# Down stage of the feed-forward parts: a block of the product in seven products in place of eight

## The reference, cut to what matters

```python
D_MODEL, SEQ, DEPTH, D_FF = 1024, 512, 2, 2816

def swiglu(x, w_gu, w_down):
    g, u = jnp.split(x @ w_gu, 2, axis=-1)
    return (jax.nn.silu(g) * u) @ w_down

for layer in range(DEPTH):
    f = swiglu(rmsnorm(h, g[N_FFN1_PRE]), ffn_w_gu[layer, 0], ffn_w_down[layer, 0])
    h = h + 0.5 * rmsnorm(f, g[N_FFN1_POST])
    # ... even layer: sparse attention and RG-LRU; odd layer: gated linear attention
    # ... cross-attention to 256 memory tokens
    f = swiglu(rmsnorm(h, g[N_FFN2_PRE]), ffn_w_gu[layer, 1], ffn_w_down[layer, 1])
    h = h + 0.5 * rmsnorm(f, g[N_FFN2_POST])
```

## Time and profile before

| | us |
|---|---|
| median of 3 runs | 2181.17 (2180.8 to 2181.19) |
| the profiled execution, its own time | 2181.75 |
| its span | 2180.0 |
| TensorE busy (PE) | 2163.3 |
| VectorE busy (DVE) | 1453.7 |
| ScalarE busy (ACT) | 1130.1 |
| GpSimd busy (POOL) | 110.4 |
| mean granted TensorE clock | 0.999 |

### The profile page before, as it was taken

The page is one execution under the profiler, slowest core; times in us unless marked ns, Lnnn a source line. Parts: engine busy times, 40 slices in busy tenths (PEclk is TensorE's granted clock), DMA queues, the critical chain, the costliest instruction groups (busy, mean ns, idle before and its releaser), DMA issues.

```text
span 2180.0 us, 36486 instructions
## 1 busy us (share of the span) xinstructions
PE 2163.3 (99%) x13768; PEld 1944.7 (89%) x13768; DVE 1453.7 (67%) x2179; ACT 1130.1 (52%) x1887; POOL 110.4 (5%) x104
## 2 busy tenths in 40 slices
PE   9999999999999999999999999999999999999998
PEld 8999888775888899998899998898889889999987
DVE  8888635798565688874388886354356567888732
ACT  6555534476554555554365555245445546555531
POOL 0000000576000000000000000000000000000000
PEclk9999999999999999999999999999999999999999
DMA  4332332221452233323323333323323422333332
GB/s 165 106 106 96 116 99 71 78 72 55 135 165 78 78 115 98 105 95 118 126 70 104 106 106 106 106 75 104 103 77 120 155 82 74 102 103 103 115 97 78
DMA packets 62017, 221.51 MB, mean 102 GB/s; under 512 B 7985, under 2 KB 8113, under 8 KB 61922
## 3 DMA queue, kind: packets, MB, share of 16 engines
q1 hardware_dynamic: 57456, 208.69, 29.4%
q10 hardware_dynamic: 4466, 11.53, 1.5%
HBM read 218.09 MB, written 2.10 MB: 101 GB/s over the span
## 4 chain that ended last, share of the span: by engine, by line
PE 91%; DVE 5%; ACT 2%; DMA 1%; POOL 1%; issue 1%; DVEq 0%; POOLq 0%; ACTq 0%
PE ps L2116 12%; PE ps L2118 12%; PE ps L2117 12%; PE ps L2212 11%; PE ps L2214 11%; PE ps L2213 11%; PE ps L481 6%; PE ps L482 5%; PE ps L483 5%; PE ps L2052 1%; DMA w_raw<-in_wstream 1%; DVE w_lo L419 1%; DVE e_sc L1776 1%; DVE e_max L1775 1%; DVE e_sc L1791 1%
## 5 line engine op out<-in xcount | busy, mean ns | idle before, releaser
L419 DVE TENSOR_TENSOR w_lo<-w_raw,w_hi 128x1024 fp32r<-128x1024 f32 x204 | 252.2, 1240 | 350.9 <-ACT w_hi L414 349.9
L414 ACT ACTIVATE w_hi<-w_raw 128x1024 fp32r<-128x1024 f32 x210 | 221.7, 1057 | 322.3 <-PE ps L2214 216.9
L2116 PE MATMUL ps<-t_hi,w_hi 128*128 128x256 f32 x1280 | 362.3, 283 | 0.0
L2118 PE MATMUL ps<-t_hi,w_lo 128*128 128x256 f32 x1280 | 362.3, 283 | 0.0
L2117 PE MATMUL ps<-t_lo,w_hi 128*128 128x256 f32 x1280 | 362.3, 283 | 0.0
L2118 PE MATMUL ps<-x_hi,w_lo 128*128 128x256 f32 x960 | 271.7, 283 | 0.0
L2117 PE MATMUL ps<-x_lo,w_hi 128*128 128x256 f32 x960 | 271.7, 283 | 0.0
L2116 PE MATMUL ps<-x_hi,w_hi 128*128 128x256 f32 x960 | 271.7, 283 | 0.0
L1498 DVE TENSOR_TENSOR w_lo<-f,w_hi 128x1024 fp32r<-128x1024 f32 x152 | 186.1, 1224 | 124.2 <-ACT w_hi L841 124.2
L481 PE MATMUL ps<-x_hi,w_hi 128*128 128x256 f32 (+1 forms) x736 | 250.7, 341 | 2.0 <-DVE x_lo L1375 1.0
L482 PE MATMUL ps<-x_lo,w_hi 128*128 128x256 f32 (+1 forms) x736 | 246.0, 334 | 0.0
(11 more groups left out here) (358 smaller groups left out, 4308.1 us busy)
## 6 DMA issues: line engine op xcount, KB each, us to landing
w_raw<-in_wstream SPq DMA_DIRECT2D x310, 512.0 KB, 3.7
w_raw_odd<-in_wstream SPq DMA_DIRECT2D x80, 512.0 KB, 3.6
tmp<-in_post_gains ACTq DMA_DIRECT2D x8, 512.0 KB, 4.5
gain_bc<-in_gains ACTq DMA_DIRECT2D x7, 512.0 KB, 3.8
h<-in_x SPq DMA_DIRECT2D x4, 512.0 KB, 6.2
c_mem<-in_mem ACTq DMA_DIRECT2D x2, 1024.0 KB, 5.5
out_dram<-h SPq DMA_DIRECT2D x3, 512.0 KB, 2.7
c_gain<-in_mem_gains ACTq DMA_DIRECT2D x2, 512.0 KB, 7.6
```

The lines of the kernel that those rows point to most:

```text
L414: nc.scalar.activation(weights(v)[0], raw(v), ACT.Copy).then_inc(w_hi_ready, 1)
L419: nc.vector.tensor_tensor(wl, raw(v), wh.bitcast(f32), ALU.subtract).then_inc(w_ready, 1)
L2116: nc.tensor.matmul(dst, wh[:, at], xh[:, b, :], start=first, stop=False, skip_group_check=True)
L2118: last = nc.tensor.matmul(dst, wl[:, at], xh[:, b, :], start=False, stop=final, skip_group_check=True)
```

## The change

In the Down stage, the first eight of the 22 inner tiles, with all 512 tokens and all 1024 columns, are seen as a product of 2x2 blocks: 256 tokens by four inner tiles, times four inner tiles by 512 columns. The four blocks of the result come from seven block products (Strassen's scheme in Winograd's form) in place of eight. Each block product has two units of 12 products. The other 14 inner tiles stay as before, as row units. `DOWN` is the order of the 28 units; 14 of them are loaded as before and split, four (of products 1 and 2) too, and the ten of products 3 to 7 are made from blocks that lie in the space of `x_hi` and `x_lo`, which the gate/up stage no longer needs.

VectorE makes the sums of weights (`first_t`, `t_second`, `t_third`, `t_fourth`), the sums of activations (`a_raw`) and the lower parts of both. Products 1, 5, 6 and 7 are copied by ScalarE out of PSUM into `f` (`down_kept`), since they go into two results; VectorE adds them to other banks (`put`). SP loads six block units, two of them ahead of unit 0. `output` is no longer used for the Down stage; each engine has a `down` of its own. Half 0 now ends ahead of the three late units of half 1.

```diff
+BLOCKS = {1: (0, 0), 2: (0, 1), 3: (1, 1)}
+DOWN = [("block", n, k) for n in (1, 2, 5) for k in range(2)] + [("row", 1, 4)]
+DOWN += [("block", 6, 0), ("block", 6, 1), ("row", 1, 5), ("block", 7, 0), ("block", 7, 1), ("row", 1, 6)]
+DOWN += [("block", 3, 0), ("block", 3, 1), ("row", 1, 7), ("block", 4, 0), ("block", 4, 1)]
+DOWN += [("row", 0, q) for q in range(4, FT // 2)] + [("row", 1, q) for q in range(8, FT // 2)]
+DOWN_FIRST = DOWN.index(("row", 0, FT // 2 - 1)) + 1
...
-    "ffn": [("gate_up", 2 * FT), ("down", FT)],
+    "ffn": [("gate_up", 2 * FT), ("down", len(DOWN))],
...
+                        places = (DOWN.index(("block", 4, 1)), DOWN.index(("block", 3, 1)), DOWN.index(("row", 0, 5)))
+                        LAST_USE.append(U[i, seg] + places[late] if kind == "ffn" else U[i, "v"] + KT - 1)
...
         def _(sp):
...
+                            if at == ("block", 1, 0):
+                                sp.wait_ge(w_free, U[i, "gate_up"] + 2 * PLAIN + 2)
+                                for k in range(2):
+                                    sp.dma_start(x_quarter(*AT12, k), block_rows(i, FT // 2 + k)).then_inc(block_in[0], 16)
+                            elif at == ("block", 5, 0):
+                                sp.wait_ge(w_free, U[i, seg] - 2 + 3)
+                                for k in range(2):
+                                    sp.dma_start(x_quarter(*AT22, k), block_rows(i, FT // 2 + 2 + k)).then_inc(block_in[1], 16)
+                            elif at == ("row", 1, 5):
+                                sp.wait_ge(prod, 5 * (SEVENS[i] + FT))
+                                for k in range(2):
+                                    sp.dma_start(x_quarter(*AT21, k), block_rows(i, 2 + k)).then_inc(block_in[2], 16)
...
         def _(act):
...
-                act_upper(i, 0)
+                form_upper(i, 1)
                 keep(it, par, K1, 0, 0)
...
+                form_upper(i, 2)
                 split_hi(act, d0 + 2)
                 pair_silu(it, par)
                 act.wait_ge(w_free, d0 + 2)
-                act_upper(i, 1)
                 split_hi(act, d0 + 3)
-                output(i, "down", FT // 2)
+                down(i)
...
+            def down_kept(i, n):
+
+                act.wait_ge(w_free, U[i, "down"] + DOWN.index(("block", (1, 5, 6, 7)[n], 1)) + 3)
+                b = 0 if n == 1 else 6
+                nc.scalar.activation(kept_place(n), ps[:, b:b + 2, :], ACT.Copy).then_inc(d_kept, 1)
+
+            def down_upper(i, p):
+
+                v = U[i, "down"] + p
+                what, n, k = DOWN[p]
+                if what == "row" or n < 3:
+                    split_hi(act, v)
+                    return
+                if n == 3:
+                    act.wait_ge(block_in[1], 32 * (nffn[i] + 1))
+                else:
+                    act.wait_ge(w_sum, 8 * nffn[i] + W_SUMS[n] + k + 1)
+                act.wait_ge(w_free, LAST_USE[v] + 3)
+                nc.scalar.activation(weights(v)[0].rearrange("p (a b) -> p a b", b=HB), x_quarter(*T_PLACE[n], k),
+                                     ACT.Copy).then_inc(w_hi_ready, 1)
+
+            def down(i):
+                act.preload_act_table(ACT.Sqrt)
+                act.wait_ge(w_free, d0 + 2)
+                act.wait_ge(a_sum, 4 * nffn[i] + A_SUMS[5])
+                form_upper(i, 5)
...
+                for p in range(len(DOWN)):
+                    if p == 1:
+                        down_kept(i, 0)
+                        act_upper(i, 4)
+                    elif p == 3:
+                        act.wait_ge(a_sum, 4 * nffn[i] + A_SUMS[6])
+                        form_upper(i, 6)
+                    elif p == 5:
+                        down_kept(i, 1)
+                        act_upper(i, 5)
+                        act.wait_ge(a_sum, 4 * nffn[i] + A_SUMS[7])
+                        form_upper(i, 7)
...
+                    if p == DOWN_FIRST - 1:
+                        for t in range(TT):
+                            post_square(i, 0, t)
+                    if p + AHEAD < len(DOWN):
+                        down_upper(i, p + AHEAD)
+                    elif d0 + p + AHEAD < NU:
+                        split_hi(act, d0 + p + AHEAD)
...
         def _(dve):
...
-                act_lower(i, 0)
+                form_lower(i, 1)
+                dve.wait_ge(prod, 5 * (s0 + FT) - 4)
+                dve.wait_ge(block_in[0], 32 * (nffn[i] + 1))
+                first_t(i, 0)
                 split_lo(dve, d0)
                 dve.wait_ge(gu_free, n0 + FT + 1)
                 gate_first(it, 1)
+                first_t(i, 1)
                 split_lo(dve, d0 + 1)
                 up_second(it, 1)
                 gate_second(it, 1)
+                form_lower(i, 2)
                 split_lo(dve, d0 + 2)
                 pair_mul(it, 1)
-                act_lower(i, 1)
+                dve.wait_ge(gu_free, n0 + FT + 2)
+                nc.vector.tensor_tensor(a_raw(5), a_block(1, 0), a_block(1, 1), ALU.add).then_inc(a_sum, 1)
                 split_lo(dve, d0 + 3)
-                output(i, "down", FT // 2)
+                down(i)
...
+            def down(i):
...
+                def t_second():
+                    dve.wait_ge(block_in[1], 32 * (nffn[i] + 1))
+                    dve.wait_ge(w_ready, d0 + DOWN.index(("block", 5, 1)) + 1)
+                    for k in range(2):
+                        t = x_quarter(*T_PLACE[6], k)
+                        nc.vector.tensor_tensor(t, x_quarter(*AT22, k), t, ALU.subtract).then_inc(w_sum, 1)
...
+                def put(b, n):
+                    part = ps[:, b:b + 2, :]
+                    nc.vector.tensor_tensor(part, part, kept_place(n), ALU.add).then_inc(d_sum, 1)
+
+                for p in range(len(DOWN)):
+                    if p == 0:
+                        form_lower(i, 5)
+                    elif p == 2:
+                        dve.wait_ge(a_sum, 4 * nffn[i] + 1)
+                        nc.vector.tensor_tensor(a_raw(7), a_block(0, 0), a_block(1, 0), ALU.subtract).then_inc(a_sum, 1)
+                        dve.wait_ge(a_sum, 4 * nffn[i] + 2)
+                        nc.vector.tensor_tensor(a_raw(6), a_raw(5), a_block(0, 0), ALU.subtract).then_inc(a_sum, 1)
+                        act_lower(i, 4)
+                    elif p == 3:
+                        t_second()
+                        form_lower(i, 6)
+                    elif p == 4:
+                        t_third()
+                    elif p == 5:
+                        act_lower(i, 5)
...
+                    if p == DOWN_FIRST - 1:
+                        half_sums(i)
+                        for t in range(TT):
+                            store_half(i, 0, t)
+                    if p + AHEAD < len(DOWN):
+                        down_lower(i, p + AHEAD)
+                    elif d0 + p + AHEAD < NU:
+                        split_lo(dve, d0 + p + AHEAD)
...
         def _(pe):
...
+                def block_part(n, k, start):
+                    v = d0 + DOWN.index(("block", n, k))
+                    pe.wait_ge(w_ready, v + 1)
+                    wh, wl = weights(v)
+                    hi, lo = a_form(n)
+                    for t in range(2):
+                        for j in range(2):
+                            at = slice(j * SEQ, (j + 1) * SEQ)
+                            ah, al = (a[:, 2 * k + j, t * P:(t + 1) * P] for a in (hi, lo))
+                            last = added(bank(banks[n] + t), ah, al, wh[:, at], wl[:, at], start and k == j == 0)
+                    last.then_inc(w_free, 1)
...
+                block_product(1, True)
+                block_product(2, True)
+                pe.wait_ge(gu_free, n0 + FT + 2)
+                block_product(5, True)
+                pe.wait_ge(d_kept, 4 * nffn[i] + 2)
+                row(1, 4, (2, 3, 0, 1), (2, 3))
+                block_product(6)
+                row(1, 5, range(TT))
+                pe.wait_ge(d_kept, 4 * nffn[i] + 3)
+                block_product(7)
+                row(1, 6, range(TT))
+                block_product(3)
+                row(1, 7, range(TT))
+                pe.wait_ge(d_kept, 4 * nffn[i] + 4)
+                block_product(4)
+                pe.wait_ge(d_sum, 4 * nffn[i] + 1)
+                for q in range(4, FT // 2):
+                    row(0, q, range(TT))
+                pe.wait_ge(d_sum, 4 * nffn[i] + 4)
+                pe.wait_ge(w_ready, d0 + len(DOWN))
+                for t in range(TT):
+                    for q in range(8, FT // 2):
+                        last = row_tile(1, q, t, False, q == FT // 2 - 1)
...
```

More of the change, by code:

```diff
@@ L67, in trunk @@
     ALU, ACT, AX = mybir.AluOpType, mybir.ActivationFunctionType, mybir.AxisListType
-    U, _ = unit_starts(parts)
-    NU = wstream.shape[0]
+    U, NU = unit_starts(parts)
     NP = len(parts)
@@ L89, in trunk @@
             c_p_lo = early.enter_context(nc.sbuf_tensor("c_p_lo", [P, 2, MT, SEQ], f32r))
```

(51 more changed lines are left out.)

145 lines of the change are left out of this document (136 added, 9 removed).

## The result

The changed kernel takes **2200.1 us** (median of six runs, 2197.6 to 2201.7) against 2181.2 (2180.8 to 2182.2): **1.0083** times the time of before, interval 1.0072 to 1.0094. It is slower, as forecast (2195, range 2180 to 2206); the forecast fell 5 us short. The profiled execution took 2199.81 us, its span 2198.1, which is 18.1 more than before.

A forecast was written before the change was run, and what follows sets the result against it. TensorE was taken as the bound, busy for 99% of the span. Products saved -21.8, copy waits +13.2, ends of feed-forward parts +17.2 and clock +5.5 gave +14.1 us, so 2195 us, range 2180 to 2206.

The forecast's parts named there:

- Saved: Down stage on TensorE: 24 products fewer at 0.2267 us, 5.44 us less in each feed-forward part, 21.8 us in four.
- Beside TensorE: Down stage, each part: 25 more VectorE instructions, some 31 us, and 13 more on ScalarE, some 14 us, hidden by the sum.
- The rival in which VectorE becomes the bound: Block phase of the Down stage: block 7 or 3 waits as well, another 2 us a part, 2203 us; chance 8%.
- the two waits: TensorE waiting for product 5's copy, 13.2 us in all, and at the ends of feed-forward parts, 17.2 us in all.
- The change from gate/up to down: Start of the Down stage: added sums and forms fall into idle time and cost nothing.
- The copy of product 5: First row unit of each Down stage: TensorE waits 3.3 us for ScalarE's copy out of PSUM, 13.2 us in four.
- The transitions: From a feed-forward part to the next part: late statistics delay TensorE 5.2 and twice 6.0 us, 17.2 in all.
- The clock: Slower TensorE clock after new stops: 1.0 us for each of four copy stops, 0.5 for each of three part ends, 5.5.
- The rival in which every stop pays in full: Every new TensorE stop costs a full slow clock stretch of 1.7 us, 12 in all, 2202 us; chance 14%.
- all seven stops: TensorE's new stops: four at the Down stages' first row units, about 3.3 us each, and three at ends of feed-forward parts.
- Sum: Whole kernel: -21.8 + 13.2 + 17.2 + 5.5 = +14.1 us against the profiled execution, median put at 2195 us.

The follow-up runs named there:

- the cheapest cure: Half 0's squares and stores moved behind the splits of the next part's units 0 and 1, against the changed kernel: 2176.5 us, 0.9977 of before.

## Why the prediction was right, and where it was short

**Saved: right.** 97.94 against 103.38 us a part with no stop in the way is 5.44, and 21.8 in four.

**Beside TensorE: right, a little too high.** 28 us more on VectorE and 12.5 on ScalarE in each part, where the sum had 31 and 14. The rival in which VectorE becomes the bound didn't come: once the two waits are gone TensorE runs through.

**The change from gate/up to down: right.** The first product starts 0.14 us later in the first part (239.68 against 239.54), inside the spread of the runs here (239.01 to 239.88).

**The copy of product 5: right.** Followed to 259.15, measured 259.18, and the steps between go as followed: VectorE's sums for block 6 from 254.78 (forecast 254.7), the copy from 258.12 (258.1). With 97.94 us for the stage without a stop, a stop costs 101.17 - 97.94 = 3.2 us in the fourth part, where the clock held, and 102.86 - 97.94 - 1.71 = 3.2 in the first: 12.9 in all, forecast 13.2. The order on ScalarE, copy behind two waiting uppers, is shown by the run that moved the copy.

**The transitions: right in place and kind, mis-sized.** Forecast 5.2 + 6.0 + 6.0 and 1.5 for the clock, 18.7; measured 5.52 + 8.10 + 7.63 = 21.3. At the first the statistics come at +10.55, forecast +10.2. At the second the store comes 12.69 us after the late units' start (1099.92), forecast 11.75, and at the third 12.21; at the second, the load of unit 3 took 4.65 us to land in place of the 3.6 I took. The rest is the clock: after the longer stop the second tile's transposes start at 1111.18, 1.1 us after its scaling ended (1110.04), and likewise at the third; in the first transition, where the clock falls too, they follow at once (364.29 after 364.23). The step also explained too little: it says that the squares stand ahead of the splits, but it counts from the end of half 0, as if the splits could not come earlier. That they stood behind a wait of their own, with unit 0 already landed, is not in it, so it would not have led to the cheapest cure.

**The clock: right in kind, some 2 us short.** Three of the four stops at the row unit were followed by a loss of 1.71 us, 5.1 us in place of 4.0, and the two later transitions lost 1.1 each, where 1.5 stood for all three. The rival in which every stop pays in full (2202) came nearest to the measured time, but by luck: it has 12 us for the clock where 7.3 were lost, and the longer transitions fill part of the difference. The Trainium skill's TensorE: Matmul & The Clock Gate, Part 1 (The HAM clock gate), makes the half clock the state that an idle array returns to. The stop filled with work, after which the clock held, agrees. What the prediction drew from it, that by it alone all seven stops would pay in full, goes too far: the clock fell at six of seven, not at that of 2.92 us, and at the transitions part of the fall cost nothing. The rule doesn't by itself tell which stop pays, since stops of the same length went both ways here.

**Sum.** -21.8 + 12.9 + 5.1 + 21.3 + 0.6 = +18.1, against +14.1.

## What to carry to other kernels

This change saved work on the bound engine and was paid for in waits, and these sat in the program order of the engines that were half idle. So, for each instruction that moves, ask what it waits for and what is queued behind it, not how long it takes. Here a wait placed one step too early held two splits for some 10 us, and through the two raw buffers two loads, and cost about as much as the products saved (21.3 against 21.8 us). Before giving such a change up, put the wait behind the work that doesn't need it, and put the bound engine's independent work (here two of four tiles) ahead of the wait.

## What the runs showed of the hardware

A single stop of TensorE in dense work can lower its clock, and the falls come in equal pieces: added up as above (one minus the granted clock), every fall at a stop read here comes to 1.70 to 1.71 us, or to 3.41 to 3.42, twice that. It is a loss only where TensorE has work: at the second transition the clock is already down while TensorE still stands (0.71 in the row from 1103), and at the first the next wait hides the fall.

Over all kernels here, stops at the first row unit of 0.35 to 1.11 us were never followed by a fall (14 stops), those of 1.57 to 1.77 us once in four, and those of 2.9 to 3.5 us in 13 of 16. The transitions' stops of 3.8 to 5.7 us came with a fall in 15 of 15, ten of them with one of twice the size. The stop of 1.44 us in the mixing part, 1.43 to 1.46 us in all kernels, had its fall in 4 of 12 profiles, with the same instructions around it. So stops of one length went both ways, and what decides between them is open. One execution of each kernel was profiled, so how often one stop of one kernel has its fall is not shown.
